# A hybrid decoder step on one core: sums of squares on VectorE, the memory's root multiplied in later, gate matmuls moved ahead of the state outputs, the GLU product ahead of the layer norm, and the last expert job split into tiles

## The reference

```python
n = _rmsnorm(h, norm1_g)
z = n @ w_in + b_in                      # u_s5 | conv_glu_in | q_mem | gate logits (3 x 1024)
# branch A: diagonal complex SSM, y = Re(C state) + D*u, zz = gelu(y)
br_s5 = (zz * jax.nn.sigmoid(zz @ s5_glu_w + s5_glu_b)) @ w_s5_proj
# branch B: GLU, causal depthwise conv of 31 taps, layer norm, silu
br_conv = c_out @ w_conv_proj
# branch C: 4 heads of attention into 256 memory tokens,
m = _rmsnorm(mem, mem_norm_g); k = m @ w_mem_k; v = m @ w_mem_v
br_xa = o.reshape(bsz, t, XA_WIDTH) @ w_xa_proj
h = h + (g[:, :, 0] * br_s5 + g[:, :, 1] * br_conv + g[:, :, 2] * br_xa) @ w_out
# PEER: 8 heads, top 16 of 16384 experts each; u and v rows of 1024 are gathered
act = jax.nn.gelu(jnp.einsum('thkd,td->thk', u_tab[experts], xb))
h = h + jnp.einsum('thk,thkd->td', gate * act, v_tab[experts])
y = _rmsnorm(h, final_norm_g)
```

## Time and profile before

| | us |
|---|---|
| median of three runs (lowest, highest) | 1919.29 (1916.39, 1919.93) |
| the profiled execution | 1918.61 |
| its span, first to last instruction | 1916.8 |
| PE busy (matmul) | 1517.8 (79%) |
| DVE busy | 1298.0 (68%) |
| ACT busy | 527.2 (28%) |
| POOL busy | 647.8 (34%) |

### The profile page before, as it was taken

The page is one execution under the profiler, slowest core; times in us unless marked ns, Lnnn a source line. Parts: engine busy times, 40 slices in busy tenths (PEclk is TensorE's granted clock), DMA queues, the critical chain, the costliest instruction groups (busy, mean ns, idle before and its releaser), DMA issues.

```text
span 1916.8 us, 22322 instructions
## 1 busy us (share of the span) xinstructions
PE 1517.8 (79%) x7779; PEld 787.3 (41%) x7779; DVE 1298.0 (68%) x3346; ACT 527.2 (28%) x1278; POOL 647.8 (34%) x605
## 2 busy tenths in 40 slices
PE   8999999998879988988888989554556675565567
PEld 7888788786334443443333434111111111111112
DVE  5998665427776766676667667766777767777755
ACT  3111133113333344343223333231122121221212
POOL 0020030004434334444344434434444434444442
PEclk9989999999989999999988999768866888677768
DMA  5453564659999999999999999999999999999997
GB/s 212 144 89 110 176 134 148 195 181 369 420 405 404 418 417 418 417 417 419 419 409 407 420 419 421 406 422 416 411 423 418 400 395 418 421 422 420 420 421 293
DMA packets 112706, 675.45 MB, mean 352 GB/s; under 512 B 12784, under 2 KB 15296, under 8 KB 42576
## 3 DMA queue, kind: packets, MB, share of 16 engines
q0 software_dynamic: 80816, 577.23, 74.0%
q1 hardware_dynamic: 31216, 95.87, 14.1%
q10 hardware_dynamic: 560, 0.92, 0.2%
HBM read 665.79 MB, written 6.21 MB: 351 GB/s over the span
## 4 chain that ended last, share of the span: by engine, by line
PE 41%; DMA 41%; issue 7%; DVE 6%; POOL 2%; ACT 2%; ACTq 0%; POOLq 0%; DVEq 0%
DMA upper<-in_peer_uv,upper 22%; DMA lower<-in_peer_uv,upper 19%; PE pair L1199 12%; PE pair L677 7%; PE pair L688 6%; PE pair L1045 4%; PE pair L791 3%; PE pair L1194 2%; DVE upper L2120 2%; PE pair L991 1%; ACT upper L1598 1%; POOL upper L653 1%; POOL lower L653 1%; DVE lower L2120 1%; PE pair L722 1%
## 5 line engine op out<-in xcount | busy, mean ns | idle before, releaser
L1199 PE MATMUL pair<-upper 64*64 64x512 f32 x2368 | 385.3, 761 | 208.1 <-ACT upper L1598 207.9
L653 POOL DMA_INDIRECT upper<-in_peer_uv,upper x324 | 363.9, 1123 | 508.3 <-PE pair L1199 415.4
L653 POOL DMA_INDIRECT lower<-in_peer_uv,upper x220 | 246.9, 1122 | 462.1 <-PE pair L1199 273.3
L1199 PE MATMUL pair<-lower,upper 64*64 64x512 f32 x1600 | 259.0, 756 | 128.6 <-ACT upper L1598 128.5
L2120 DVE CUSTOM_DVE_ANT_0 upper<-upper 128x1024 f32<-128x1024 f32 x172 | 210.8, 1225 | 122.2 <-DMA upper<-in_peer_uv,upper 122.1
L2120 DVE CUSTOM_DVE_ANT_0 upper<-upper,lower 128x1024 f32<-128x1024 f32 x152 | 186.2, 1225 | 127.5 <-DMA upper<-in_peer_uv,upper 126.7
L1199 PEld LDWEIGHTS pair<-upper 64*64 64x64 f32 x2368 | 91.0, 166 | 407.2 <-ACT upper L1598 273.7
L1598 ACT ACTIVATE upper<-upper 128x64 f32<-128x64 f32 (+2 forms) x543 | 155.4, 338 | 307.5 <-DVE upper L2136 307.3
L1045 PE MATMUL pair<-lower 128*128 128x288 f32 x704 | 214.0, 434 | 3.9 <-ACT upper L1456 3.9
L1406 ACT ACTIVATE upper<-upper 128x4 f32<-128x4 f32 (+1 forms) x141 | 41.9, 297 | 634.8 <-DVE upper L2120 634.7
L2120 DVE CUSTOM_DVE_ANT_0 lower<-lower,upper 128x1024 f32<-128x1024 f32 x116 | 142.1, 1225 | 89.8 <-DMA lower<-in_peer_uv,upper 89.8
(11 more groups left out here) (425 smaller groups left out, 1781.9 us busy)
## 6 DMA issues: line engine op xcount, KB each, us to landing
lower<-in_w_in SPq DMA_DIRECT2D x64, 512.0 KB, 4.8
lower<-in_peer_q SPq DMA_DIRECT2D x28, 512.0 KB, 7.9
lower<-in_proj SPq DMA_DIRECT2D x48, 256.0 KB, 6.6
lower<-in_w_out SPq DMA_DIRECT2D x16, 512.0 KB, 4.8
upper<-in_peer_uv,upper POOLq DMA_INDIRECT x324, 12.8
upper<-in_cache_k SPq DMA_DIRECT2D x8, 512.0 KB, 4.3
upper<-in_cache_v SPq DMA_DIRECT2D x8, 512.0 KB, 4.4
lower<-in_peer_uv,upper POOLq DMA_INDIRECT x220, 13.5
```

What stands on the lines that cost most here:

```text
L653: pool.indirect_dma_start(row(g), None, a["peer_uv"], bass.IndirectOffsetOnAxis(ap=idx[:, n % 8, j:j + 1], axis=0)).then_inc(row_in[g % RI ...
L1199: mm = pe.matmul(acc[put, r, :], d[own, 0:64], v[own, h * 512:(h + 1) * 512], start=begun, stop=ended)
```

## The change

1. Start: constants are loaded first, x after `k0`'s weights, the S5 parameters after `v1`'s. DVE scales the memory by its column weight alone, and PE multiplies keys at once; DVE adds the eight squares of memory and of x, and PE sums over partitions once for each, after `k2`. The root of the memory's mean square is multiplied into the keys by DVE (during the S5 constants) and into the values by ACT, as a per-partition scale, when it empties `v`; for the latter two small matmuls give the sums per token as columns.
2. Gates: gate 4 is begun two steps ahead of y0, and six gate steps follow y0 and y1 each before the next job; gates 11 and 12 come from behind `at0`/`as1` and `ao0`. The y jobs get pairs of their own.
3. GLU: all four sigmoids come before the root of the layer norm, and DVE multiplies `zg` before the reciprocal.
4. Last job: rows 0 to 9 are tiled and belong to the block before, rows 10 to 15 stay whole; `add_block` of that block moves from row 10 to row 12.

```diff
-JOBS = (["ssm", "ssx"] + [f"k{c}" for c in range(4)] + ["v"]
+JOBS = (["k0", "k1", "k2", "ssx", "ssm", "k3", "v"]
...
-        + [GATES[0], "ss_s"] + GATES[1:4] + ["as0", "y0"] + GATES[4:7] + ["y1"] + GATES[7:10] + ["y2", GATES[10]]
-        + ["at0", "as1", GATES[11], "ao0", GATES[12]]
-        + ["at1", GATES[13], "ao1"] + GATES[14:16]
-        + ["ss_p"] + GATES[16:18] + ["ss_o"] + GATES[18:21] + ["ss_x"] + GATES[21:]
+        + [GATES[0], "ss_s"] + GATES[1:4] + ["as0", GATES[4], "y0"] + GATES[5:9] + ["y1"] + GATES[9:12] + ["y2", GATES[12]]
+        + ["at0", "as1", GATES[13], "ao0", GATES[14]]
+        + ["at1", GATES[15], "ao1", GATES[16]]
+        + ["ss_p"] + GATES[17:19] + ["ss_o"] + GATES[19:22] + ["ss_x"] + GATES[22:]
...
+SPLIT = 10
+def whole(n, j):
+    return EXPERTS[n][0] == TILES or (n == NJ - 1 and j >= SPLIT)
+def block_of(n, j):
+    return BLOCK_OF[n] - int(n == NJ - 1 and j < SPLIT)
...
+            sp.dma_start(const, a["consts"]).then_inc(consts_in, 16)
             sp.dma_start(memT, a["mem_t"]).then_inc(mem_in, 16)
-            sp.dma_start(nT, a["x_t"]).then_inc(x_in, 16)
-            sp.dma_start(const, a["consts"]).then_inc(consts_in, 16)
-            sp.dma_start(s5p, a["s5_pack"]).then_inc(s5_in, 16)
...
             for j in range(4):
                 load(f"k{j}", a["w_mem_k"][j])
+                if j == 0:
+                    sp.dma_start(nT, a["x_t"]).then_inc(x_in, 16)
             for j in range(4):
                 load(f"v{j}", a["w_mem_v"][j])
+                if j == 1:
+                    sp.dma_start(s5p, a["s5_pack"]).then_inc(s5_in, 16)
...
-            ps = begin("ssm")
-            for k in range(KD):
-                pe.wait_ge(msq_ok, k + 1)
-                mm = pe.matmul(ps[:, 0, 0:MEM], ones, msq[:, k, :], start=(k == 0), stop=(k == KD - 1))
...
+            for j in range(3):
+                keys_of_memory(j)
+            ps = begin("ssx")
+            pe.wait_ge(sums_ok, 2)
+            for h in range(2):
+                mm = pe.matmul(ps[:, h, 0:HT], ones, xsq[:, 0, h * HT:(h + 1) * HT], start=True, stop=True)
...
+            pe.matmul(ps[:, 0, 0:MEM], ones, msq[:, 0, :], start=True, stop=True)
+            for m in range(2):
+                mm = pe.matmul(ps[:, 1, 4 * m:4 * m + 4], msq[:, 0, m * P:(m + 1) * P], ones[:, 0:4], start=True, stop=True)
...
+            keys_of_memory(3)
...
-            woven(out_of_states(0, 0, 14), gate_by_gate(4, 7), 4)
-            woven(out_of_states(1, 14, 28), gate_by_gate(7, 10), 4)
-            woven(out_of_states(2, 28, 32), gate_by_gate(10, 11))
+            between = gate_by_gate(4, 13)
+            for i, (lo, hi) in enumerate(PARTS):
+                if i < 2:
+                    alone(between, 2)
+                woven(out_of_states(i, lo, hi), between, 0 if i == 2 else 4)
+                if i < 2:
+                    alone(between, 6)
...
-            glu_gate(0)
-            glu_gate(1)
+            for j in range(HALF):
+                glu_gate(j)
             emptied(act, "lnv")
             act.activation(lrs, lrs, ACT.Sqrt).then_inc(lr_ok, 1)
-            glu_gate(2)
-            glu_gate(3)
...
+            dve.wait_ge(consts_in, 16)
+            for k in range(KD):
+                dve.wait_ge(msq_ok, k + 1)
+                ts(memT[:, k, :], memT[:, k, :], c("gm", k), None, ALU.mult).then_inc(m_ok, 1)
+            for v, ready in ((msq, msq_ok), (xsq, xsq_ok)):
+                for k in range(1, KD):
+                    dve.wait_ge(ready, k + 1)
+                    link(tt(v[:, 0, :], v[:, 0, :], v[:, k, :], ALU.add))
+                dve.sem_inc(sums_ok, 1)
...
+            dve.wait_ge(rms_ok, 2)
+            dve.reciprocal(mcol, mcol).then_inc(key_step, 1)
...
             dve.sem_inc(epad_ok, 1)
+            link(dve.reciprocal(mr, mr))
+            for j in range(HEADS):
+                emptied(dve, f"k{j}")
+                tt(kT[:, j, :], kT[:, j, :], mr, ALU.mult).then_inc(key_step, 1)
...
+            for j in range(HALF):
+                emptied(dve, f"glu{j}")
+                tt(zg[:, j, :], zg[:, j, :], zz[:, j, :], ALU.mult).then_inc(zg_ok, 1)
             dve.wait_ge(lr_ok, 1)
             link(dve.reciprocal(lrs, lrs))
             for j in range(HALF):
                 stt(cact[:, j, :], cact[:, j, :], c("lg", j), lrs, ALU.mult, ALU.mult).then_inc(lnx_ok, 1)
-            for j in range(HALF):
-                emptied(dve, f"glu{j}")
-                tt(zg[:, j, :], zg[:, j, :], zz[:, j, :], ALU.mult).then_inc(zg_ok, 1)
...
-                    if j == 10 and n and n == BLOCKS[BLOCK_OF[n]][0]:
+                    if j == (12 if n == NJ - 1 else 10) and n and n == BLOCKS[BLOCK_OF[n]][0]:
                         add_block(BLOCK_OF[n] - 1)
```

More of the change, by code:

```diff
@@ L606, in _ @@
             pool.memset(masked_q, 0.0).then_inc(q_zero, 1)
-            for n in ("k0", "k1", "k2", "k3", "v"):
-                emptied(pool, n)
+            emptied(pool, "v")
+            pool.wait_ge(key_step, 1 + HEADS)
             pool.dma_start(o["mem_k"], kT).then_inc(mem_out, 16)
@@ L702, in _, with keys_of_memory @@
             pe.wait_ge(made, 2)
-            ps = begin("ssm")
-            for k in range(KD):
-                pe.wait_ge(msq_ok, k + 1)
-                mm = pe.matmul(ps[:, 0, 0:MEM], ones, msq[:, k, :], start=(k == 0), stop=(k == KD - 1))
-            mm.then_inc(full[0], 1)
-            ps = begin("ssx")
-            for k in range(KD):
-                pe.wait_ge(xsq_ok, k + 1)
-                for h in range(2):
-                    mm = pe.matmul(ps[:, h, 0:HT], ones, xsq[:, k, h * HT:(h + 1) * HT],
-                                   start=(k == 0), stop=(k == KD - 1))
-            mm.then_inc(full[1], 1)
-            for j in range(4):
+            def keys_of_memory(j):
                 w = loaded(f"k{j}")
@@ L880, in woven, with alone @@
                         next(large, None)
-                for _ in large:
-                    pass
+            def alone(large, count):
+                for _ in range(count):
+                    next(large)
             scores(0)
@@ L905, in _ @@
             mm.then_inc(full[JOB["ss_p"][0]], 1)
-            gates(16, 18)
-            between = gate_by_gate(18, 21)
+            gates(17, 19)
+            between = gate_by_gate(19, 22)
             for _ in sample_values():
@@ L1187, in _ @@
                         nth = V_USERS[g][1]
-                        begun = n == BLOCKS[b][0] and j == mine[0]
-                        ended = n == BLOCKS[b][-1] and j == mine[-1]
+                        begun = g == 0 or block_of((g - 1) // TOPK, (g - 1) % TOPK) != b
+                        ended = g == TOPK * NJ - 2 or block_of((g + 1) // TOPK, (g + 1) % TOPK) != b
+                        if begun and b >= 2:
+                            pe.wait_ge(acc_step, b - 1)
                         pe.wait_ge(diag_ok, nth)
@@ L1214, in _, with key_out @@
                 act.activation(xsq[:, k, :], nT[:, k, :], ACT.Square).then_inc(xsq_ok, 1)
-            emptied(act, "ssm")
-            act.activation(mr, mr, ACT.Sqrt).then_inc(rms_ok, 1)
+            def key_out(j):
+                ps = filled(act, f"k{j}")
+                act.activation(kT[:, j, :], ps[:, 0, 0:MEM], ACT.Copy).then_inc(drained(f"k{j}"), 1)
+            for j in range(3):
+                key_out(j)
             emptied(act, "ssx")
             act.activation(xr, xr, ACT.Sqrt).then_inc(rms_ok, 1)
+            emptied(act, "ssm")
+            act.activation(mr, mr, ACT.Sqrt)
+            act.activation(mcol, mcol, ACT.Sqrt).then_inc(rms_ok, 1)
             act.wait_ge(s5_in, 16)
             act.activation(at(tab, G), s5p[:, 0:G], ACT.Tanh, scale=1.0 / 16).then_inc(s5_scan_in, 1)
-            for j in range(4):
-                ps = filled(act, f"k{j}")
-                act.activation(kT[:, j, :], ps[:, 0, 0:MEM], ACT.Copy).then_inc(drained(f"k{j}"), 1)
+            key_out(3)
             act.wait_ge(epad_ok, 1)
@@ L1628, in _ @@
             tt, ts, stt = dve.tensor_tensor, dve.tensor_scalar, dve.scalar_tensor_tensor
+            dve.wait_ge(consts_in, 16)
[7 more added lines that the diff above has]
+                dve.sem_inc(sums_ok, 1)
+            ps = filled(dve, "ssx")
+            ts(halves(xr), two(ps), 1.0 / D, RMS_EPS, ALU.mult, ALU.add).then_inc(drained("ssx"), 1)
             ps = filled(dve, "ssm")
[L1631 to L1632 removed]
+            ts(mr, ps[:, 0, 0:MEM], 1.0 / D, RMS_EPS, ALU.mult, ALU.add)
+            ts(mcol, ps[:, 1, 0:8].rearrange("p (m c) -> p m c", m=2)[:, :, 0], 1.0 / D, RMS_EPS, ALU.mult, ALU.add
+               ).then_inc(drained("ssm"), 1)
             dve.wait_ge(rms_ok, 1)
[L1634 to L1639 removed]
             link(dve.reciprocal(xr, xr))
```

63 lines of the change are left out of this document (30 added, 33 removed).

## The result

The changed kernel takes 1898.29 us (median of 4 runs, 1897.39 to 1900.55), the kernel before on the same chip 1918.44 (1916.39 to 1919.93): ratio 0.9897 [0.988, 0.9915], 20.1 us faster. Run again beside the last experiment it took 1899.0 (1897.43 to 1900.28), ratio 0.9907 [0.989, 0.9923]. The forecast was 1897.5, the range of 1890 to 1906. The first is the slowest of its four executions, the second the fastest of its four.

What follows compares the result with a forecast made beforehand. TensorE was taken to bound the front until about 440 us, the DMA engines the gathers, then a tail. Gains 7.2 + 10.1 + 2.1 + 2.4 = 21.8 us gave 1896.8, stated as 1897.5 us for the median; range 1890 to 1906.

Steps and rivals of the forecast that it cites:

- (a): Start: PE begins on k0 without waiting for the root, sums take fewer passes, u jobs begin at 40.2, not 47.4: -7.2 us.
- (c): GLU: gated products ahead of the norm's reciprocal let P0.0 start sooner: -2.1 us, bounds 0.8 and 3.5.
- (d): Last job: rows 0 to 9 tiled, so PE idles sooner and DVE's block addition sets the end: -2.4 us.
- The first gather 20 us earlier: Sign to look for at the end of the front: the first gather's issue moves 20 us earlier.
- no wait, or 1.4 us; I take none: S5 constants at PE's 16-column products: DVE's later delivery costs PE no wait, or 1.4 us; none was charged.
- rival 1: Cover or clock fails in one or two terms (constants, y part, tail): 1907 us, one alone 1902; chance 0.20.
- (b): y0 to y2: gate steps cover DVE's draining, removing two waits (5.2 us) and low-clock stretches (1.9 and 3.0): -10.1 us.
- If the clock falls all the same, -5.2: Weaker case for the y jobs: waits shrink but the low clock still follows, so the gain is only 5.2 us.
- 0 to 1.3: GLU: stall in us at the fifth P job, because the norm's root, reciprocal and scalings come later.
- Rival 2: Gathers swallow the front's gain, so only the tail's 2.4 us stays: 1916 us; chance 0.06.
- Rival 3: Slower: a lower clock in the trunk beside the gathers (500 to 1200 us) makes PE the bound: 1933 us; chance 0.02.
- Rival 4: The y reordering fails because y1 still shares y0's pair of banks; given no chance of its own.

Runs made afterwards that it cites:

- the last experiment: Changed kernel with ET drained before ScalarE issues the copies of T and the norm's reciprocal and scalings spread between DVE's P products: 1894.66 us, ratio 0.9884.
- the four kernels with the old start: The kernel before (1918.46 us), and it with only the gates around y moved (1908.31), only GLU products first (1916.12) or only the last job tiled (1915.89).
- those with the new start: Kernel before with only the start changed (1912.88 us), changed kernel (1898.29), and changed kernel with five/three (1902.99) or eight/no (1906.01) gate steps ahead of/behind y0, y1.
- the first y kernel: Changed kernel with five gate steps ahead of y0 and y1 and three behind each, instead of two and six: 1902.99 us, ratio 0.992.
- (a) alone: Kernel before with only the start changed (load order, k0 to k2 ahead of the sums, squares added on DVE, root multiplied in later): 1912.88 us, ratio 0.9969.
- the kernel with eight steps ahead: Changed kernel with eight gate steps ahead of y0 and y1 and none behind, instead of two and six: 1906.01 us, ratio 0.9945.
- (d): Kernel before with only the last job's rows 0 to 9 tiled and the block's addition behind dot 12: 1915.89 us, ratio 0.999.
- (c) alone: Kernel before with only the GLU products moved ahead of the layer norm's reciprocal: 1916.12 us, ratio 0.9987.

## Why the prediction was right, and where it was not

It was right in sign, size and, but for one step in (a), mechanism: 1897.5 forecast, 1898.3 and 1899.0 measured. That it is within 1 us is in part luck: (a) fell short by over 1 us and (c) and (d) were off by about half a microsecond, one up and one down, which is within the noise. "The first gather 20 us earlier" is 16.2 us in the first profile and 19.3 in the second. Term by term:

- **(a) -7.2 forecast, about -6 measured** (-5.9 alone by ratio; -6.2 between the means of `scores(0)` above; -4.3 and -7.5 in the two profiles of the changed kernel). The reckoning up to the `u` jobs held to 0.1 us, 40.15 against 40.2, and so did the judgement on the constants, "no wait, or 1.4 us; I take none": 1.25 us are left. The step that failed is the unwritten one behind it: the 7.2 us at the `u` jobs were carried to the end whole, as if everything behind the constants kept its distance, and only the scan after them was looked at. In its place the stretch from the first 16-column product to `ag2` grew from 16.6 to 17.4 us in the mean. The cover I watched was DVE's; the one that gave way was ScalarE's. `ET`'s drain stands behind ScalarE's issue of the copies, an order which cost the four kernels with the old start 0.22 to 1.76 us of wait, and those with the new start 0.70 to 3.22. POOL's U loads (L612 to L616) are tied to the constants, so they came later by 1.26 us (97.52 to 98.78) while PE came earlier by 7.1; the copies now follow at once on the last U load. Then landings take 6.4 to 8.4 us instead of 2.0 to 3.1, and in four of five profiles the issues take longer in sum. The later the copies were issued, the less of it: from 108.3 to 109.1 us on, 6.4 to 8.4 us to land (four profiles); from 110.83, 4.0 to 4.5 (the first y kernel); from 113.0 or later, 2.0 to 3.1. That the drain behind the issue costs PE time is shown, by the kernels that swap them; they gain more (2.8 us at `scores(0)` in the mean) than (a) had lost, because they also take away the wait that the kernel before had; that it is the U loads that slow the copies is read from the order in time only, since no run moved those.
- **In one profile of five the passes of `ag2` ran slower as well**, 16.59 us against 14.9, with the granted clock at 0.70 in 115 to 120 us. This is what rival 1 described for another place: a standstill of 2.06 us and a low clock behind it. In (a) alone and in the kernel with eight steps ahead the standstill was 3.2 us and the passes took 14.91, so here too a standstill brought the low clock in some executions and not in others.
- **(b) -10.1 forecast; -10.4 by ratio, -9.3 between the moments.** 0.3 us was to be left of each wait; none is. The clock's share comes out by difference: waits of 5.0 us explain half of 9.3, and the clock of 1.00 where it was 0.56 the other 4.3 (2.8 and 3.7 us against (a) and (d)); the 4.9 forecast were somewhat too many, and the mechanism is as said. "If the clock falls all the same, -5.2" did not come. The Trainium skill (TensorE: Matmul & The Clock Gate, A second HAM failure mode: psum-queue depth-cycling) tells of a kernel in which frequent short stops make the clock swing. Two waits of 1.2 to 1.3 us, which are short but not frequent, left it at 1.00 here, and of two of 2.5 us one was followed by a swing.
- **(c) -2.1 forecast, -2.5 by ratio, -2.6 between the moments.** The wait of P0.0 shrank by 2.0, as said. The clock behind it was full, which the bounds allowed, and the stall at the fifth P job 0.95 us, inside "0 to 1.3". The sum took the case in which the shorter wait still brings the low clock, and it didn't; its 2.1 are close only because the clock's gain and the stall nearly cancel, which is luck. By the rows it is 2.0 (wait) + 1.7 (the first two P jobs, 5.25 us before and 3.56 in (c) alone) - 0.95 (stall) = 2.7. Load and root took 1.98 us from 328.00 to 329.98, as before. The drain of 1.38 us that the Trainium skill gives besides the load (ScalarE: Activation LUTs, What ACT_TABLE_LOAD costs) has no room in this trace either.
- **(d) -2.4 forecast, -1.9 measured**, by ratio and in both profiles of the changed kernel. As forecast, DVE's addition of the block sets the end. The low clock did appear, on the first tiled rows (3.61 us for 16 passes of 64x64 tiles at 1871.50, 3.60 for the next 32), but for the residual and the two last rows it was full again.
- **Rival 1** fell in the places that it named: PE didn't wait for the constants, no low clock came back in the y part, and none ruled the last rows. **Rival 2** fell: what the front gained arrived at the end, 1484.47 us from first gather to end before and 1482.6 now, the tail's share alone. **Rival 3** fell: the clock is 0.95 in 600 to 1200 us. **Rival 4** fell: no y pass waits.

## What to carry to other kernels

When a stretch of one engine's work is pulled forward, list for every engine what is queued ahead of the instruction it will wait for, DMA issues included: a queue order that cost little while the engine was late becomes the next limit, and a transfer that used to run alone may meet another. Let the operation somebody waits for go ahead of issues nobody waits for yet. A wait removed in the TensorE-bound stretch can be worth more than its length where a low clock follows it (5.0 us of waits were worth 7.8 to 9.3), so price it from the rows behind the wait as well as from the wait; and read more than one profile before a microsecond or three are explained, since the same kernel differed by 3 us in one place alone.

## What the runs showed of the hardware

- The issue of one 32 to 224 KB copy on ScalarE's queue takes 0.5 to 0.6 us as a rule, and in single cases 1.0 to 2.37 us when it comes right behind POOL's sixteen loads of 16 and 128 KB. ScalarE runs nothing else meanwhile: ahead of the drain it is idle for 4.85 us in the kernel before and for 6.61 in (a).
- The same seven copies land in 2.0 to 3.1 us by themselves and in 6.4 to 8.4 when issued right behind those loads. That the loads are the cause is read from the order in time.
- The 64 16-column passes take 8.84 to 11.24 us from one execution to another, with identical instructions. The granted clock is 1.00 at their start and falls to 0.50 on the way, and the time goes with the moment of the fall: in 102 to 104 us it is still 1.00 in the execution with 8.84 us (20 passes in these 2 us) and already 0.50 in the one with 11.24 (12 passes).
- Waits of PE of 0.7 to 1.8 us left the clock at 1.00. Waits of 2.1 to 3.6 us were followed by about 0.50 in most places and executions and by full speed in others (2.59 us ahead of a gate, 3.2 us ahead of `ag2`, twice).
